# Last projection of a two-layer kernel turned from feature-major to token-major, with three borders between its stages rearranged

## The reference

```python
# layer 1: attention (compressed, selected and window keys), then SwiGLU
h = x + nsa_mixer(rmsnorm(x, mix_norm_g), ...)       # 16 heads in 4 groups
h = h + swiglu(rmsnorm(h, ffn_norm_g), ffn_w_in, ffn_w_out)
y1 = rmsnorm(h, final_norm_g)
# layer 2: an mLSTM branch (ya) and a pooling branch (yb), merged by gates into m
x2 = rmsnorm(y1, norm_pre_w_2)
...
out = y1 + rmsnorm(m @ w_out_2, norm_post_w_2)       # w_out_2 is 2048 x 2048
```

## Time and profile before

| what | value |
|---|---|
| median of 3 timed runs | 2166.55 us (2165.16 to 2167.64) |
| the profiled execution, its own time | 2169.18 us |
| its span in the profile | 2167.4 us |
| mean granted TensorE clock | 0.994 |
| PE busy | 2141.8 us (99%) |
| DVE busy | 1415.0 us (65%) |
| ACT busy | 1050.6 us (48%) |
| weights in | 387 MB, 182 GB/s over the span |

### The profile page before, as it was taken

The page is one execution under the profiler, slowest core; times in us unless marked ns, Lnnn a source line. Parts: engine busy times, 40 slices in busy tenths (PEclk is TensorE's granted clock), DMA queues, the critical chain, the costliest instruction groups (busy, mean ns, idle before and its releaser), DMA issues.

```text
span 2167.4 us, 34467 instructions
## 1 busy us (share of the span) xinstructions
PE 2141.8 (99%) x12316; PEld 1885.4 (87%) x12316; DVE 1415.0 (65%) x1845; ACT 1050.6 (48%) x1375; POOL 68.9 (3%) x143
## 2 busy tenths in 40 slices
PE   9999999999999999999999999999999999999996
PEld 8888889888888888888888888888888888888885
DVE  7766665766666666645556777867777676556565
ACT  6564554554444444444445455444454454444453
POOL 1001221000000000000000000000000000000001
PEclk9999999999999999999999999999999999999998
DMA  8585333555556556555565455545555555555552
GB/s 299 185 276 177 123 118 117 190 191 183 193 174 203 184 193 190 175 198 193 186 191 182 146 175 193 182 160 189 189 178 176 173 185 189 188 186 194 187 191 97
DMA packets 108596, 395.53 MB, mean 182 GB/s; under 512 B 12306, under 2 KB 12322, under 8 KB 108512
## 3 DMA queue, kind: packets, MB, share of 16 engines
q1 hardware_dynamic: 106272, 386.97, 54.0%
q0 software_dynamic: 2096, 7.33, 1.0%
q10 hardware_dynamic: 144, 0.04, 0.0%
HBM read 389.83 MB, written 2.13 MB: 181 GB/s over the span
## 4 chain that ended last, share of the span: by engine, by line
PE 97%; DVE 1%; ACT 1%; issue 0%; DMA 0%; POOL 0%; SPq 0%; ACTq 0%
PE set L1435 52%; PE set L1443 27%; PE set L1461 4%; PE set L1467 2%; PE misc L1578 1%; PE set L1421 1%; PE set L1423 1%; PE set L1422 1%; PE set L1549 1%; PE misc L1651 1%; PE set L1407 1%; PE set L1409 1%; PE set L1408 1%; PE misc L1637 1%; PE misc L1787 0%; PE misc L1653 0%
## 5 line engine op out<-in xcount | busy, mean ns | idle before, releaser
L757 DVE TENSOR_TENSOR w_hl<-raw,w_hl 128x1024 fp32r<-128x1024 f32 x729 | 886.5, 1226 | 564.1 <-ACT w_hl L469 557.7
L469 ACT ACTIVATE w_hl<-raw 128x1024 fp32r<-128x1024 f32 x729 | 761.3, 1056 | 781.3 <-PE set L1443 360.6
L1435 PE MATMUL set<-x_hl,w_hl 128*128 128x512 f32 x3520 | 859.8, 394 | 1.5 <-DVE t L1136 1.5
L1435 PEld LDWEIGHTS set<-x_hl,w_hl 128*128 128x128 f32 x3520 | 646.7, 189 | 126.3 <-DVE t L1136 1.9
L1443 PEld LDWEIGHTS set<-x_hl,w_hl 128*128 128x128 f32 x3520 | 454.0, 191 | 18.8 <-issue 0.9
L1443 PE MATMUL set<-x_hl,w_hl 128*128 128x256 f32 x3520 | 463.9, 284 | 0.0
L1435 PE MATMUL set<-f_hl,w_hl 128*128 128x512 f32 x704 | 168.7, 391 | 0.0
L476 ACT ACTIVATE cross<-set 128x512 f32<-128x512 f32 (+1 forms) x150 | 88.1, 587 | 138.7 <-PE set L1435 126.4
L1435 PEld LDWEIGHTS set<-f_hl,w_hl 128*128 128x128 f32 x704 | 129.2, 188 | 24.9
L1443 PEld LDWEIGHTS set<-f_hl,w_hl 128*128 128x128 f32 x704 | 90.8, 191 | 3.7
L1461 PE MATMUL set<-w_hl,x_hl 128*128 128x512 f32 x384 | 92.9, 391 | 0.0
(11 more groups left out here) (304 smaller groups left out, 1755.1 us busy)
## 6 DMA issues: line engine op xcount, KB each, us to landing
raw<-in_weights SPq DMA_DIRECT2D x730, 512.0 KB, 4.1
bias_g<-bias POOLq DMA_DIRECT2D x4, 572.0 KB, 3.7
cur<-in_cur POOLq DMA_DIRECT2D x4, 535.0 KB, 3.6
h<-in_x SPq DMA_DIRECT2D x4, 512.0 KB, 7.1
bias<-u_dram POOLq DMA_DIRECT2D x1, 2048.0 KB, 14.5
out<-y_t SPq DMA_DIRECT2D x4, 512.0 KB, 2.8
w<-in_w POOLq DMA_DIRECT2D x1, 256.0 KB, 5.4
vm<-in_causal POOLq DMA_DIRECT2D x1, 192.0 KB, 3.4
```

The costliest lines, as they stand in the source:

```text
L469: a(high, whole, ACT.Copy).then_inc(hi_ready, 1)
L757: tt(low, whole, high.bitcast(F32), ALU.subtract).then_inc(lo_ready, 1)
L1435: last = mm(out[:, f * 2 * S:(f + 1) * 2 * S], w[:, 0, c], hl[:, kt, :, :], start=first and k == 0, stop=low_first, skip_group_check=True)
```

## The change

1. **Last projection.** `gemm` with `unit_features` becomes `block_tokens` (and `block_tokens_apart` for the last chunk, which finishes tokens 0 to 127 first and signals `half_out`). The weights are laid out by blocks in place of halves, a token's 2048 outputs now lie along one partition.
2. **Norm.** ACT squares each 128x512 piece straight from PSUM and sums along the row (`accum_out`); the variance is a number per token (128x1). The gain is a row, `post_row`, loaded by one POOL DMA that repeats 8 KB on all partitions (1 MB). DVE multiplies the piece by it (`take_out`).
3. **First layer's output.** `h` is scaled in block 0 and turned to token-major by 32 transposes on PE (`rows_by_tokens`) into the four small PSUM banks, two of which ACT copies out to `h_t`.
4. **End.** Five pieces are finished on DVE by one instruction each (`finish`), three by ACT's scaling and POOL's addition. Eight DMAs of 256 KB, each of 2 KB rows, in place of four.
5. **Borders.** Border (a): `transposes(0, 0)` one chunk later, and ACT's `exps(0, 1)` ahead of it. Border (b): operands and squares spread between splits. Border (c): `taken` is incremented before the norms, two new semaphores guard the normed values, the gates' transposes stand one chunk later, and `g_broadcast` is cut in four, one part after each of four chunks.

```diff
-        for n, ready, count in ((0, y_ready, 1), (1, y_ready, 2), (2, y2_ready, 1), (3, y_ready, 3)):
+        for t, q, ready, count in ((0, 0, y_ready, 1), (0, 1, y_ready, 2), (0, 2, y2_ready, 1), (1, 0, y_ready, 3),
+                                   (0, 3, y2_ready, 2), (1, 1, y_ready, 4), (1, 3, y2_ready, 3), (1, 2, y_ready, 5)):
             sp.wait_ge(ready, count)
-            sp.dma_start(d["out"][:, 4 * n:4 * n + 4, :], y_t[:, 4 * n:4 * n + 4, :]).then_inc(y_out, 16)
+            sp.dma_start(piece(d["out"], t, q), piece(y_t, t, q)).then_inc(y_out, 16)
...
+        pool.wait_ge(chunks_done, C_WO)
+        pool.dma_start(post_row[:, :], bass.AP(tensor=d["post"].tensor, offset=0, ap=[[0, P], [1, D]])).then_inc(post_in, 16)
+        for n, (t, q) in enumerate(((0, 2), (0, 3), (1, 3))):
+            pool.wait_ge(y_scaled, n + 1)
+            g.tensor_tensor(piece(y_t, t, q), piece(y_t, t, q), h_t[:, t, q - 2, :], ALU.add).then_inc(y2_ready, 1)
...
+        splits(Pos(C_WO + 3 * NB), NB, squares_out(2) | {2: lambda: a(stat[:, 0, 0:1], ones[:, 0:1], ACT.Sqrt)})
+        square_out(3, 0)
+        post_root(0)
+        square_out(3, 1)
+        act.wait_ge(post_ready, 1)
+        act.wait_ge(out_taken, 5)
+        scale_out(0, 2)
+        act.wait_ge(out_taken, 7)
+        scale_out(0, 3)
+        post_root(1)
+        act.wait_ge(post_ready, 2)
+        act.wait_ge(out_taken, 8)
+        scale_out(1, 3)
...
+        def take_out(n, t):
+            dve.wait_ge(out_squared, 2 * n + t + 1)
+            tt(piece(y_t, t, n), sets[(B_WO + n) % 2][:, t * BLK:(t + 1) * BLK], post_row[:, n * BLK:(n + 1) * BLK],
+               ALU.mult).then_inc(out_taken, 1)
...
+        def finish(t, q, rows):
+            stt(piece(y_t, t, q), piece(y_t, t, q), post[:, t:t + 1], rows, ALU.mult, ALU.add).then_inc(y_ready, 1)
...
-                own.link(summed(t1[:, 2:4, :], number + 1, the_set + 1, NO_CROSS_ML))
+                summed(t1[:, 2:4, :], number + 1, the_set + 1, NO_CROSS_ML).then_inc(taken, 1)
+                dve.wait_ge(taken, number + 2)
...
-                tt(t1[:, 2:4, :], t1[:, 2:4, :], rows(PRE, 2), ALU.mult).then_inc(taken, 1)
+                tt(t1[:, 2:4, :], t1[:, 2:4, :], rows(PRE, 2), ALU.mult).then_inc(first_normed, 1)
...
         def attention(gi, slot):
             n = slot // 2
             if slot % 2 == 0:
+                if n == 2 and isinstance(gi, int) and gi == 0:
+                    transposes(gi, 0)
...
+            for t in range(TT):
+                for f in range(FT):
+                    kt = (n * FT + f + KT // 2) % KT
+                    last = nc.tensor.transpose(m[2 * t + n % 2][:, f * P:(f + 1) * P], h[:, kt, t * P:(t + 1) * P], ident[:, :])
+            last.then_inc(ht_done, 1)
...
+                if n == 3 and j == NB - 1:
+                    chunk(at, j, wait, lambda: block_tokens_apart(at, j, out, m_hl, kts))
+                else:
+                    chunk(at, j, wait, lambda: block_tokens(at, j, out, m_hl, kts, j == 0))
+                if n * NB + j in (3, 5, 7, 9):
+                    rows_by_tokens((n * NB + j - 3) // 2)
```

More of the change, by code:

```diff
@@ L582, in attention @@
             if slot % 2 == 0:
+                late = isinstance(gi, int) and gi == 0 and n == 2
+                if late:
+                    exps(gi, 1)
                 if real(gi, n - 2):
                     take_pt(gi, n - 2)
-                if real(gi, n - 1):
+                if real(gi, n - 1) and not late:
                     exps(gi, n - 1)
@@ L721, in _ @@
             merge(i)
-        def scale_y(n):
-            act.wait_ge(taken, B_WO + 2 * n + 2)
-            for kt in range(n * FT, (n + 1) * FT):
-                last = a(y_t[:, kt, :], out_t[:, kt, :], ACT.Copy, scale=gains[:, POST, kt:kt + 1])
-            last.then_inc(y_scaled, 1)
-        def square_out(n):
-            act.wait_ge(taken, B_WO + 2 * n + 2)
-            square(sq[:, :, :], out_t[:, n * FT:(n + 1) * FT, :], n + 13).then_inc(sq_ready, 1)
-        for n in range(4):
-            splits(Pos(C_WO + n * NB), NB, {2: lambda n=n: scale_y(n - 1), 1: lambda n=n: square_out(n - 1)} if n else None,
-                   B_WO + 2 * n, B_WO)
@@ L737, in _, with take_rows, square_out @@
-        act.wait_ge(stats_ready, 16)
-        for k in range(2):
-            act.wait_ge(taken, B_WO + 7 + k)
-            a(sq[:, 2 * k:2 * k + 2, :], out_t[:, 3 * FT + 2 * k:3 * FT + 2 * k + 2, :], ACT.Square).then_inc(out_sq, 1)
-        root(POST, 5)
-        scale_y(3)
+        def take_rows(n):
+            act.wait_ge(ht_done, n + 1)
+            for t in range(TT):
+                last = a(h_t[:, t, n, :], m[2 * t + n][:, :], ACT.Copy)
+            last.then_inc(ht_taken, 1)
+        def square_out(n, t):
+            if n < 3:
+                act.wait_ge(chunks_done, C_WO + (n + 1) * NB)
+            elif t == 0:
+                act.wait_ge(half_out, 1)
+            else:
+                act.wait_ge(chunks_done, CHUNKS)
+            if n > 0:
+                act.wait_ge(out_squared, 2 * n + t - 1)
+            a(flat(sq[:, 2 * t:2 * t + 2, :]), sets[(B_WO + n) % 2][:, t * BLK:(t + 1) * BLK], ACT.Square,
+              accum_out=post_sq[:, t, n:n + 1]).then_inc(out_squared, 1)
@@ new lines, in scale_out, with post_root, squares_out @@
+        def scale_out(t, q):
+            a(piece(y_t, t, q), piece(y_t, t, q), ACT.Copy, scale=post[:, t:t + 1]).then_inc(y_scaled, 1)
+        def post_root(t):
+            act.wait_ge(post_var_ready, t + 1)
+            a(post[:, t:t + 1], post_var[:, t:t + 1], ACT.Sqrt).then_inc(post_ready, 1)
+        def squares_out(n):
+            return {t: lambda t=t: square_out(n, t) for t in range(TT)}
+        splits(Pos(C_WO), NB, {4: lambda: take_rows(0), 6: lambda: take_rows(1)})
+        splits(Pos(C_WO + NB), NB, squares_out(0))
@@ L1360, in _ @@
             merge(i)
-        def out_taken(n, half):
-            kt = n * FT + half * HT
-            unit = B_WO + 2 * n + half
-            summed(out_t[:, kt:kt + HT, :], unit, unit, NO_CROSS_ML).then_inc(taken, 1)
-        def first_layer_out(kt):
-            stt(h[:, kt, :], h[:, kt, :], gains[:, FINAL, kt:kt + 1], row(FINAL), ALU.mult, ALU.mult)
-        for n in range(4):
-            splits(Pos(C_WO + n * NB), NB, {j: lambda kt=n * FT + j: first_layer_out(kt) for j in range(FT)} |
-                   ({5: lambda n=n: add_squares(sq, 0, 16 + n, n == 1)} if n else {}),
-                   half=lambda n=n: out_taken(n, 0))
-            out_taken(n, 1)
@@ L1376, in _, with first_layer_out @@
-        variance(5, width=S)
-        dve.wait_ge(rms_ready, 5)
-        for n in (0, 1, 3):
-            dve.wait_ge(y_scaled, n + 1)
-            part = y_t[:, n * FT:(n + 1) * FT, :]
-            own.link(tt(part, part, rows(POST), ALU.mult))
-            tt(part, part, h[:, n * FT:(n + 1) * FT, :], ALU.add).then_inc(y_ready, 1)
+        def first_layer_out(j):
+            for kt in (2 * j + KT // 2, 2 * j + KT // 2 + 1):
+                kt %= KT
+                last = stt(h[:, kt, :], h[:, kt, :], gains[:, FINAL, kt:kt + 1], row(FINAL), ALU.mult, ALU.mult)
+            last.then_inc(first_out_ready, 1)
@@ L1730, in pooled @@
             def pooled():
-                pe.wait_ge(taken, number + 1)
+                if first:
+                    pe.wait_ge(first_normed, 1)
+                else:
+                    pe.wait_ge(taken, number + 1)
                 pe.wait_ge(cur_in, i * 16 + 16)
```

163 lines of the change are left out of this document (113 added, 50 removed).

## The result

The changed kernel takes 2156.42 us (median of five runs, 2156.41 to 2156.56) against 2167.64 for the kernel before in the same series (five runs, 2165.16 to 2167.78). The ratio is 0.995, 95% interval 0.994 to 0.9961. The direction was right, the size was not: 11.0 us above the forecast of 2145.4 and outside its range.

A forecast was written before the change was run, and what follows sets the result against it. PE, busy 99% of the span, was taken to bound the kernel. Gains 3.7 + 1.7 + 2.7 + 3.4 - 1.75 + 11.4 = 21.15 us off 2166.55 gave 2145.4; own range 2143.5 to 2147, over cases 2142.5 to 2150.5.

The forecast's parts named there:

- Border (a): Transposes of head 0, first attention group: 2.02 us pause waiting for POOL and 1.7 us of low clock go, 3.7 us gained.
- Border (b): PE's wait for a split behind ACT's operand and square: the pause goes, 1.74 us gained.
- Border (c): PE's waits for `taken` and for the gate transposes: 2.67 us gained, with 0.16 us of the gates' wait remaining.
- The broadcast: Gates' broadcast matmuls cut into four pieces: the low clock goes, 3.41 us gained, bounds 0 and 3.41.
- The matmuls cost what they cost: Step at the broadcast: each of four pieces takes a quarter of the 3.5 us, 0.86 us.
- The last projection: Chunks at 2.73 us gain 1.7, 32 added transposes of `h` cost 3.4: net loss 1.75 us, no waits.
- The tail: From PE's last matmul to the end of the span: falls from 20.7 to 9.3 us, 11.4 gained.
- 240 GB/s and a tail of 12.4 us: Estimate from the Trainium skill for 256 KB output pieces, 1.1 us each; the midway slow-drain rival, 2148.5, chance 0.07.
- If the timed runs lacked a low stretch of the profiled one, the price is the same and counts here.: Last clause of the rival that a low clock stays or comes anew: one stretch costs 3.4, 2148.8, chance 0.12.
- The change doesn't do what it says at the borders: Rival: all pauses and both low stretches stay, only tail and projection count; 2156.9, chance 0.02.
- Taking the same 21.15 off 2166.55: Last step of the sum: the gain reckoned on the profiled execution is taken off the median, giving 2145.4.

The follow-up runs named there:

- pad96: The changed kernel with 96 bytes of unused filler per partition behind `rtmp` instead of none; 2149.13 us, ratio 0.9914 to the kernel before.
- bc_whole: The changed kernel with 32 bytes of filler and the gates' broadcast in one piece of sixteen matmuls instead of four pieces; 2147.43 us.
- bc_two: The changed kernel with 32 bytes of filler and the gates' broadcast in two pieces of eight matmuls instead of four pieces; 2146.99 us.
- drain: The changed kernel with 32 bytes of filler, DVE doing `finish(0, 1)` ahead of `post_variance(1)` and `take_out(3, 1)`; 2146.60 us against 2146.21 without the reordering.
- borders: The kernel before with only the three rearranged borders, its last projection and end as they were, addresses as before; 2158.94 us, ratio 0.9967.
- before_pad32: The kernel before with 32 unused bytes of filler per partition; 2169.86 us, ratio 1.0014.
- a_back: The changed kernel with 32 bytes of filler and border (a) put back as it was before; 2148.45 us.
- x128: The changed kernel with 128 bytes of filler ahead of `x_hl` and 96 behind `rtmp`; 2167.94 us, ratio 1.0006 to the kernel before.

## Why the prediction failed

Measured against `pad96`, in which PE's products turn as before, the steps can be read one by one. The numbers are how much earlier PE comes to the next stage than in the profiled execution before.

- **Border (a)**: 3.7 us, predicted 3.7. Pause and low clock went, and no later wait took their place.
- **Border (b)**: 1.8, predicted 1.74. **Border (c)** with the gates: 2.8, predicted 2.67. The 0.16 us that I left for the gates didn't show.
- **The broadcast**: 1.95, predicted 3.41. The mechanism was right, its size was not: "The matmuls cost what they cost" is the step. Each piece costs some 0.4 us beyond its quarter, where it stands between matmuls of full height. A pause ahead is not needed for the low clock: `bc_whole` and `bc_two` have none there and a low clock.
- **The last projection**: a loss of 1.6, predicted 1.75; 90.86 us long against 90.8.
- **The tail**: 11.5 gained, predicted 11.4. SP's pieces of 256 KB ran as the trace's 512 KB pieces had let expect, at 0.65 us each; the prediction's estimate of 240 GB/s and a tail of 12.4 us for pieces of this size is not borne out. This window of the changed kernel answers to the earlier trace rows; only the microsecond ahead of it had a hole, which `drain` only moved:

```profile
2149.50:2154.00 4.50, 0.00 (x0) 0.00 (x0) 1.04 (x2) 0.00 (x0) 2.15 (x2) 0.55 1.05 403
2148.50:2149.50 1.00, 0.00 (x0) 0.00 (x0) 1.00 (x3) 0.28 (x1) 1.00 (x2) 1.00 0.12 43
```

Together, with 0.1 us from ahead of border (a), 20.2 us of the 21.15, and the profiled execution of `pad96` is 2148.88 where 2148.0 was predicted for that of the change. Of the rivals one came true in part, in its last clause: "If the timed runs lacked a low stretch of the profiled one, the price is the same and counts here." That the measured 2156.4 lies beside the 2156.9 of "The change doesn't do what it says at the borders" is chance: all pauses and both low stretches are gone.

The rest of the miss is in the last step of the sum, "Taking the same 21.15 off 2166.55". The 21.15 holds 5.1 us for the two low stretches of the profiled execution, 1.7 and 3.41, and the median execution does not have that much to lose. The kernel before spreads over 5.9 us (2163.47 to 2169.39 in sixteen runs), while none of the kernels that lack both its pauses and its row of sixteen small matmuls spreads over more than 0.8. The granted clock on record for each of its timed runs follows the time: 0.997 in the four of 2163.5 to 2164.9 us that have it, 0.994 in all over 2169. The profiled execution, 2169.18 less 5.1, would be 2164.1 without low clock, which is where the runs with 0.997 are. So the median of 2166.55 lost only about 2.5 us to the low clock, 2.6 less than the profiled execution. The borders show the same: 2164.1 less their pauses (2.0, 1.8 and 2.8), plus 1.5 for the four pieces, is 2159.0, and `borders` takes 2158.94. Where the low clock stands in the timed runs is not shown, for only the profiled executions place it; `before_pad32` and `a_back` show that it changes from one execution to the next.

The account from 2145.4: +2.6 for that, +0.9 for the terms, +0.25 from profile to median of `pad96`, +7.3 for the addresses: 2156.4. The 0.9, 0.25 and 7.3 are read off measured times; that the 2.6 is low clock rests on the low clock as just worked out.

What remains open is why the difference acts. The rows show that it does, in both kinds of operand and with either sign, and that 512 and 256 columns answer differently (at -64 the one is slower and the other faster than at 0). They don't show by what mechanism. I tried seven differences, all multiples of 32 bytes, with 32-bit operands only; that the rule repeats after 256 bytes rests on a move by 1024 (`pad96` against the kernel before), while 128 did not repeat it (`x128`).

## What to carry to other kernels

When a change alters the size or order of on-chip tiles, "the rest stays as it is" is a claim about addresses too: list the start of every matmul operand before and after, and compare one untouched stage's length in both traces before explaining anything else. In a kernel that PE bounds, try a few fillers for their own sake; here they were worth nearly twice what the change itself brought (20.8 us against 11.2). And a difference between the profiled execution and the median carries over to the new kernel only if its cause does.

## What the hardware showed that I had not expected

- A matmul's turn depends on where its operands start in SBUF, and in all sixteen kernels here it goes by the difference between the starts of the moving and the stationary operand: with `f_hl` moving, for 512 plus 256 columns, 0.3457 us at +64 bytes, 0.3481 at 0, 0.3526 at -96, which is 2%. Over the changed kernel, the same instructions took from 2135.63 to 2167.94 us. The Trainium skill, "SBUF — State Buffer", section Operand start alignment, asks of an operand's start only that it is a multiple of the element size, and says that this is about legality and not speed; that leaves room for what the runs show.
- TensorE's clock fell to the 1.2 GHz level with PE busy and no pause just ahead: 2.2 us into sixteen matmuls with 8 rows, for 6.83 us (`bc_whole`), and 1.3 us behind eight of them, for 3.41 (`bc_two`); with four at a time and a full chunk between, in none of twelve profiled executions.
- The same stretch of code ran at the 1.2 GHz level in one execution and not, or half as long, in another: 3.41 us behind the pause of border (a) in the kernel before, none in `before_pad32` and `a_back`; 6.82 and 3.41 us at the sixteen small matmuls.
- Among matmuls of full height, a piece of four with 8 rows costs about 0.4 us beyond its quarter.
- With several in flight, output DMAs of 256 KB ran at 403 GB/s, the 402 of the earlier trace rows for 512 KB.
